# One step of a hybrid diffusion model with a mixture of experts: expert blocks of 32 tokens in four column groups, and every weight piece through a staging buffer

## What is computed

```
scores = sigmoid(x @ router_w);  sel = scores + router_b          # 16 experts in 4 groups
# the best group, in it the best 2 experts; weights = their scores, normed to sum 1
xb  = rows of x, sorted by expert
yb  = (silu(xb @ w_gate[e]) * (xb @ w_up[e])) @ w_down[e]         # 1024 -> 1024 -> 1024, f32
y   = for each token: sum of its 2 rows of yb, each by its weight
```

## Time and profile before

| | us |
|---|---|
| median of 3 runs | 1455.94 (1453.58 to 1458.22) |
| span of the profiled execution | 1449.7 |
| the profiled execution's own time | not told by the page; the median is 6.2 above the span |
| PE busy | 1358.5 (94% of the span) |
| PE L2222 (gates), L2233 (down) busy | 405.8, 212.7 |
| DVE, ACT, POOL busy | 433.9, 265.5, 234.1 |
| HBM | 282 MB read, 33 MB written |

### The profile page before, as it was taken

The page is one execution under the profiler, slowest core; times in us unless marked ns, Lnnn a source line. Parts: engine busy times, 40 slices in busy tenths (PEclk is TensorE's granted clock), DMA queues, the critical chain, the costliest instruction groups (busy, mean ns, idle before and its releaser), DMA issues.

```text
span 1449.7 us, 26021 instructions
## 1 busy us (share of the span) xinstructions
PE 1358.5 (94%) x10242; PEld 850.3 (59%) x10243; DVE 433.9 (30%) x913; ACT 265.5 (18%) x401; POOL 234.1 (16%) x280
## 2 busy tenths in 40 slices
PE   5898999978999999999969999999999999999975
PEld 3688778756787666664434455555555455554532
DVE  4792860375622412104462000000000000000065
ACT  3305012244125000000111111111111111111102
POOL 0043402200000000000005013003122222222320
PEclk9899899998999999999989999999999999999997
DMA  7459622345430212413168818917949999999993
GB/s 302 152 136 386 140 69 66 81 147 181 170 111 10 87 44 73 172 46 145 44 249 330 342 29 340 395 29 292 396 155 396 389 398 380 403 380 403 377 402 132
DMA packets 91756, 318.07 MB, mean 219 GB/s; under 512 B 11920, under 2 KB 12304, under 8 KB 91440
## 3 DMA queue, kind: packets, MB, share of 16 engines
q1 hardware_dynamic: 72304, 268.77, 48.9%
q0 software_dynamic: 10608, 34.19, 8.0%
q10 hardware_dynamic: 8784, 14.24, 3.2%
HBM read 281.99 MB, written 33.06 MB: 217 GB/s over the span
## 4 chain that ended last, share of the span: by engine, by line
PE 79%; DMA 8%; DVE 5%; issue 3%; ACT 2%; SPq 2%; POOL 0%; POOLq 0%; DVEq 0%; ACTq 0%
PE ps L2222 22%; PE ps L1762 11%; PE ps L2233 11%; PE ps L1750 10%; DMA expert_w<-in_w_down 5%; PE ps L2132 5%; PE ps L2183 4%; PE ps L1854 2%; PE ps L1937 2%; DMA expert_w<-in_w_up 2%; SPq L553 1%; PE ps L2228 1%; PE ps L2212 1%; PE ps L1777 1%; DMA x_sorted<-h,router_ints 1%
## 5 line engine op out<-in xcount | busy, mean ns | idle before, releaser
L2222 PE MATMUL ps<-expert_w,x_block_t 128*64 128x256 f32 x3584 | 405.8, 383 | 10.6 <-issue 6.7
L2222 PEld LDWEIGHTS ps<-expert_w,x_block_t 128*64 128x64 f32 x3584 | 257.2, 138 | 159.1 <-issue 33.7
L2233 PE MATMUL ps<-expert_w,act_t 128*64 128x512 f32 x896 | 212.7, 602 | 4.1 <-DMA expert_w<-in_w_down 3.7
L1762 PE MATMUL ps<-h_t,weight_ring 128*128 128x320 f32 x640 | 179.0, 436 | 0.1
L1762 PEld LDWEIGHTS ps<-h_t,weight_ring 128*128 128x128 f32 x640 | 121.6, 191 | 54.2 <-issue 7.6
L1750 PE MATMUL ps<-h_t,weight_ring 128*128 128x320 f32 x512 | 148.8, 454 | 2.8 <-ACT h_t L730 2.8
L1661 DVE TENSOR_TENSOR activations<-silu_tmp,ps 128x256 f32<-128x256 f32 x56 | 23.6, 422 | 375.7 <-ACT silu_tmp L948 375.6
L1750 PEld LDWEIGHTS ps<-h_t,weight_ring 128*128 128x128 f32 x512 | 102.0, 201 | 46.7 <-issue 9.3
L2233 PEld LDWEIGHTS ps<-expert_w,act_t 128*64 128x64 f32 x896 | 58.3, 137 | 101.4 <-issue 81.4
L673 POOL COPY expert_w<-staged 128x1024 f32<-128x1024 f32 x42 | 43.8, 1043 | 416.8 <-PE ps L2222 315.9
L1682 DVE COPY y_block<-ps 128x512 f32<-128x512 f32 x25 | 17.3, 692 | 187.5 <-PE ps L2233 187.5
(11 more groups left out here) (355 smaller groups left out, 1309.1 us busy)
## 6 DMA issues: line engine op xcount, KB each, us to landing
expert_w<-in_w_down SPq DMA_DIRECT2D x128, 512.0 KB, 13.6
weight_ring<-in_stream SPq DMA_DIRECT2D x98, 512.0 KB, 5.0
expert_w<-in_w_gate SPq DMA_DIRECT2D x58, 512.0 KB, 11.3
expert_w<-in_w_up SPq DMA_DIRECT2D x58, 512.0 KB, 12.3
staged<-in_w_gate SPq DMA_DIRECT2D x28, 512.0 KB, 13.9
gathered<-in_w_gate SPq DMA_DIRECT2D x28, 512.0 KB, 15.9
gathered<-in_w_up SPq DMA_DIRECT2D x28, 512.0 KB, 16.5
x_sorted<-zero POOLq DMA_DIRECT2D x18, 512.0 KB, 15.0
```

The source lines that it names most:

```text
L1762: last = mm(pair(job)[:, a, :], w[:, k, :], h_t[:, k, a * HALF:(a + 1) * HALF], start=(k == 0), stop=(k == KD - 1))
L2222: last = mm(ps[MB * g:MB * g + MB, 2 * half + w, 0:256], x_blk_t[:, 2 * kp + k2, :], rows[:, at_col:at_col + 256], start=(kp == 0 and k2 = ...
L2233: last = mm(ps[MB * half:MB * half + MB, 4, :], act_t[:, 4 * (f // 4) + 2 * (f % 2) + f // 2 % 2, :], w_slot[3 * f + 2][:, 4 * half:4 * ha ...
```

## The change

A block has MB = 32 rows. With the counts above that is 48 blocks (in the order of the experts 2, 7, 1, 7, 1, 5, 2, 4, 2, 3, 2, 3, 2, 3, 2, 2). PE runs each product in four column groups of 32 stationary columns and 256 moving columns. The transposes of x and of the activations are made by DVE (32x32 blocks, with the weights stored on the host in the matching order), so PE has no transposes in the loop and ACT no copies. The down product of a block runs one block later, after the gates of the next. All 24 pieces of an expert are staged in 8 buffers and copied by POOL; of the last expert, 16 are staged and the 8 of w_down go straight to their slots. The last 4 blocks are kept in `y_last`, and there are three buffers for gathered rows, which no longer serve as staging buffers. In the diff the parts of SP, POOL, ACT, DVE and PE follow in this order; `load_x` and `store_y` are four DMAs each, of 32 rows by 1 KB, and `add_some(n)` does n half rows of the gathered sum (a product or an addition).

```diff
-MB = 64
+MB = 32
-STAGED = 10
+FG = 4
+GW = D // FG
+LASTN = 4
+STAGES = 8
+PIECES = 3 * KF
...
+            for p in range(STAGES // 2, PIECES):
+                if p >= STAGES:
+                    sp.wait_ge(slot_filled, PIECES + (p + 1 - STAGES))
+                load_piece(second, p)
             with sp.Fori(2, EXPERTS - 1) as n:
-                next_expert(n, STAGED)
+                e = sp.value_load(rint[0:1, bass.ds(n + EXPERT, 1)], min_val=0, max_val=EXPERTS - 1)
+                for p in range(PIECES):
+                    sp.wait_ge(slot_filled, n * PIECES + (p + 1 - STAGES))
+                    load_piece(e, p)
+            for p in range(2 * KF):
+                sp.wait_ge(slot_filled, last_e * PIECES + (p + 1 - STAGES))
+                load_piece(e, p)
+            for f in range(KF):
+                sp.wait_ge(down_done, b * KF + (f + 1))
+                sp.dma_start(piece[2 * KF + f][:, :], w_experts[bass.ds(e, 1), 2 * KF + f, :, :].rearrange("a p n -> p (a n)"))\
+                    .then_inc(last_in[f], 16)
...
+            def fill(n, pieces):
+                b = pool.value_load(rint[0:1, bass.ds(n + START, 1)], min_val=0, max_val=NBLK)
+                for p in range(pieces):
+                    s = p % STAGES
+                    pool.wait_ge(stage_in[s], n * (16 * PIECES // STAGES) + 16 * (p // STAGES + 1 - PIECES // STAGES))
+                    pool.sem_inc(stage_full, 1)
+                    if p < 2 * KF:
+                        pool.wait_ge(gu_done, b * (2 * KF) + (p + 1))
+                    else:
+                        pool.wait_ge(down_done, b * KF + (p + 1 - 2 * KF))
+                    pool.sem_inc(slot_free, 1)
+                    nc.gpsimd.tensor_copy(piece[p][:, :], stage[s]).then_inc(slot_filled, 1)
+            with pool.Fori(1, EXPERTS - 1) as n:
+                fill(n, PIECES)
+            with pool.Fori(EXPERTS - 1, EXPERTS) as n:
+                fill(n, 2 * KF)
-            pool.wait_ge(y_stored, stored * 32 + 32)
+            pool.wait_ge(y_stored, limit * (16 * FG))
...
+            with act.Fori(2, NBLK) as i:
+                with act.If(i < limit):
+                    for h in range(2):
+                        act.wait_ge(gu_done, i * (2 * KF) + (h + 1) * KF)
+                        act.wait_ge(prod_ready, i * 2 + h)
+                        take_gate_half(h)
+                    act.wait_ge(xt_copied, i + 2)
+                    load_x(i * MB + 2 * MB)
+                    act.wait_ge(y_copied, i + 1)
+                    store_y(i * MB - MB)
...
+            with dve.Fori(2, NBLK) as i:
+                with dve.If(i < limit):
+                    dve.wait_ge(silu_ready, i * 2 + 1)
+                    take_prod(0)
+                    dve.wait_ge(x_blk_in, i * (16 * FG) + 16 * FG)
+                    dve.wait_ge(gu_done, i * (2 * KF) + 2 * KF)
+                    turn_x(x_blk[:, :])
+                    dve.wait_ge(silu_ready, i * 2 + 2)
+                    take_prod(1)
+                    dve.wait_ge(prod_ready, i * 2 + 2)
+                    dve.wait_ge(down_done, i * KF)
+                    turn_act()
+                    dve.wait_ge(y_stored, i * (16 * FG))
+                    copy_y()
...
+            for u, (beside, amid, behind) in enumerate(((0, 0, 4), (2, 3, 3), (2, 3, 3))):
+                take_prod(0)
+                add_some(beside)
...
+                turn_x(x_blk[:, :])
+                take_prod(1)
+                add_some(amid)
+                dve.wait_ge(down_done, limit * KF + u * KF)
+                turn_act()
+                take_last(u)
+                vec.nop().then_inc(y_copied, 1)
+                add_some(behind)
+            dve.wait_ge(down_done, limit * KF + (LASTN - 1) * KF)
+            take_last(LASTN - 1)
...
+            with pe.Fori(2, NBLK) as i:
+                with pe.If(i < blocks):
+                    pe.wait_ge(xt_copied, i + 1)
+                    gate_half(0, lambda p: pe.wait_ge(slot_filled, e * PIECES + (p + 1)))
+                    pe.wait_ge(prod_ready, i * 2)
+                    gate_half(1, lambda p: pe.wait_ge(slot_filled, e * PIECES + (p + 1)))
+                    pe.wait_ge(act_ready, i)
+                    pe.wait_ge(y_copied, i)
+                    down(lambda p: pe.wait_ge(slot_filled, before * PIECES + (p + 1)))
```

More of the change, by code:

```diff
@@ L238, in hybrid_step @@
[L238 to L243, removed]
+        rms2 = at("row_rms", gone + 24 * 320 + 3520 + 448, [P, 8 * CH])
+        rw = at("router_w_sb", gone + 24 * 320 + 3520 + 640, [P, KD, EXPERTS])
+        assert gone + 24 * 320 + 3520 + 640 + 512 <= small_end
@@ new lines, in hybrid_step @@
+        w_slot = [at(f"expert_w{s}", end - s * 4096, [P, D]) for s in range(PIECES)]
+        piece = [w_slot[n] for n in SLOT_OF]
+        pick_t = at("last_tokens_t", end - 3 * 4096, [P, CH, P])
+        x_blk = at("x_block", qs0, [P, GW])
+        x_blk_t = at("x_block_t", qs0 + 1024, [P, KD, MB])
+        act_t = at("act_t", qs0 + 2048, [P, KF, MB])
+        y_blk = at("y_block", qs0 + 3072, [P, GW])
+        silu = at("silu_tmp", qs0 + 4096, [P, P])
+        acts = at("activations", qs0 + 4608, [P, 2, P])
@@ L248, in hybrid_step @@
-        assert end + 8192 <= top[0] and len(stage) == STAGED and qs0 + 40960 <= end - 23 * 4096
+        stage = [at("staged0", end + 4096, [P, D])[:, :], sm[:, b_at:b_at + D]] \
+            + [at(f"staged{2 + i}", ring0 + 12288 + i * 4096, [P, D])[:, :] for i in range(3)] \
+            + [at(f"staged{5 + i}", qs0 + 5632 + i * 4096, [P, D])[:, :] for i in range(3)]
+        assert end + 8192 <= top[0] and len(stage) == STAGES and qs0 + 40960 <= end - 23 * 4096
         fin = [at(f"final{i}", pool0 + (10 + i) * 4096, [P, D]) for i in range(CH)]
@@ L325, in hybrid_step @@
         blocks_done = sem("blocks_done")
[L326 removed]
+        got_in = [sem(f"got_in{s}") for s in range(3)]
         pick_ready = sem("pick_ready")
@@ L573, in _ @@
+            for f in range(KF):
+                sp.wait_ge(last_in[f], 16)
+                sp.sem_inc(slot_filled, 1)
             for c in range(CH):
@@ L2238, in _, with down, landed @@
+            def down(filled):
+                for f in range(KF):
+                    filled(2 * KD + f)
+                    for g in range(FG):
+                        last = mm(ps[MB * g:MB * g + MB, 4, 0:GW], act_t[:, f, :], piece[2 * KD + f][:, GW * g:GW * g + GW],
+                                  start=(f == 0), stop=(f == KF - 1))
+                    last.then_inc(down_done, 1)
+            def landed(p):
+                pe.wait_ge(first_in[p], 16)
             pe.wait_ge(act_took, h2_job("L", CH - 1) + 1)
@@ L2254, in _ @@
[L2254 to L2264 removed]
+            gate_half(0, landed)
+            gate_half(1, landed)
+            pe.wait_ge(act_ready, 1)
@@ L2303, in _ @@
             last.then_inc(pick_turned, 1)
+            pe.wait_ge(act_ready, blocks)
+            pe.wait_ge(y_copied, blocks)
+            down(lambda p: pe.wait_ge(slot_filled, EXPERTS * PIECES + (p + 1 - PIECES)))
             pe.wait_ge(pick_taken, 1)
-            def add_last(c, u):
+            for c in range(CH):
                 cv = 0 if c < SCH else 1
-                pe.wait_ge(y_last_ready, 2 * u + cv + 1)
-                for half in range(2):
-                    rows = slice(MB * half, MB * half + MB)
-                    last = mm(ps[:, 2 * (c % 2) + half, :], pick_t[rows, u, c, :], y_last[rows, u, cv, :],
-                              start=(u == 0), stop=(u == 1))
-                return last
```

447 lines of the change are left out of this document (166 added, 281 removed).

## The result

| | before | changed |
|---|---|---|
| median, us | 1455.21 (1453.58 to 1458.22, 4 runs) | 1479.33 (1474.15 to 1485.02, 4 runs) |
| span of the profiled execution | 1449.7 | 1483.2 (its own time 1485.02) |

The ratio is 1.0181 (95% interval 1.0138 to 1.0223): slower by 24 us. The forecast was 1468, in the right direction and half as large (12 us); the time lies inside the range of 1443 to 1495 and that of the likeliest case, 1460 to 1482.

What follows compares the result with a forecast made beforehand. It took PE, then DMA, to bound the expert stage, DVE the end. Copy loop's end 1395 us (6 for the clock included), 67 for the end gives 1462, plus 6.2 gives 1468 us; range 1443 to 1495.

Steps and rivals of the forecast that it cites:

- a period above 11 us: Sign against the forecast: a block in the first large expert was to take 10.4 us on PE, not over 11.
- Copy loop's end: POOL's last weight copy: 1051 + 284.5 + 48 + 5 = 1389 us, with 6 us for the clock 1395.
- 192 x 0.054 = 10.4 us a block: PE's time for a 32-row block: 192 matmul records at 54 ns, no transposes and no wait for silu.
- a rival (11.7 us a block): Four column groups miss full pace, waiting at each piece: 61 ns a record, total 1490 us; chance 0.1.
- 864 + 52 + 5 x 10.4: Start of the second large expert's last gates: first large expert's at 864, 52 us step, five blocks; 968 us.
- 6 for the clock: PE at half clock after idle waits: 2 us at each of three PE-bound places, 6 us in all.
- From there DMA never waits: After the third large expert's last block starts, at 1051 us, DMA was to be busy without a pause.
- x and y at 2.0 us a block: DMA cost of a block's loads and stores: 2.0 us, bounds 1.2 and 3.0; 48 us over 24 blocks.
- The end, 67 us: From the copy loop's end at 1395: gathers, DVE's chain of sums to 1443, then the rest to 1462 us.
- the rival with a hidden tail: Gathered sums fit between PE's last blocks, so the end takes 57 us, not 67; total 1458 us; chance 0.14.
- 6.2 us around the span: The median was put 6.2 us above the profiled span: 1462 becomes 1468 us.
- The traffic goes by bytes: Rival: x and y cost DMA 1.2 us a block instead of 2.0; total 1446 us, faster; chance 0.2.

Runs made afterwards that it cites:

- the first series: The changed kernel as it is, first group of four runs against the kernel before: 1479.33 us, ratio 1.0181; run again later, 1476.61 us, ratio 1.0159.
- the late and the extra load: Two edits of the changed kernel: PE's second table load moved behind the gates, 1467.49 us; an unused third load at the loop's head, 1495.64 us.
- the five early gathers: The changed kernel with five gathers issued among the last expert's 16 copies: 1470.6 us, ratio 1.0099.
- four more buffers: The changed kernel with 12 staging buffers instead of 8: 1452.57 us, ratio 0.9984; with late load and five gathers too, 1429.46 us, ratio 0.9823.
- the other repairs: The changed kernel with PE's second load behind the gates, 1467.49 us, or five gathers among the last copies, 1470.6 us; both together 1454.76 us.

## Why the prediction was half right

The direction was right, and most of the mechanism; four terms of the copy loop's sum were not, and they left the forecast at 12 of the 24 us measured. The first of them, the loop turn, had no term at all, and the prediction had named a period above 11 us as a sign that it was wrong. By its own steps, in the profiled execution of the first series:

- **Copy loop's end, 1395 forecast, 1413.4 measured.** Four errors, two of which cancel.
  - *The loop turn was costed at nothing.* The step "192 x 0.054 = 10.4 us a block" has 11.45 in its place: 7, 5 and 3 blocks, 15 x 1.05 = 16 us. The last gates of the first large expert start at 873.2 instead of 864; 7.4 of these 9.2 us are the turn, the rest is the lower clock and late pieces in the first two blocks. Shown by the late and the extra load. The kernel before had one load and slower matmuls: its PE-bound blocks hid one load and two alike. I had the price as a rival (11.7 us a block) with 0.1, but for another reason.
  - *The small expert's down product was left out of the step* "864 + 52 + 5 x 10.4". The 52 held (51 us), but 6.2 and 5.6 us follow it: 12. I had put 6 for the clock instead, in all.
  - *"From there DMA never waits"* was wrong: some 12 us of standstill in the fourth large expert, and shorter dips later.
  - *x and y at 2.0 us a block* was too much; the DMA-bound stretch from 1078.0 took 335.4 us, and less 284.5 for the pieces, 12 of standstill and 5 for issue, landing and copy this leaves 33.9 / 24 = 1.4 a block. 24 x 0.6 is 14 us less. Of the 1.4 only 0.9 is the traffic, in its own queue; the rest is shorter dips and slower pieces, some 13 us in all for which the sum had no term. So the 338 us forecast for the stretch were right by two errors.
  - Sum: 1395 + 16 + 12 - 6 + 12 - 14 = 1415.
- **The end, 67 us.** 69.8 from the last copy's end, and not the 57 of the rival with a hidden tail. The mechanism was right: gathers behind the copies, DVE as the chain, x's transpose behind the rows. The trace shows the order, and the five early gathers show that their place costs time.
- **6.2 us around the span.** The changed kernel's profiled execution has 1485.02 - 1483.2 = 1.8. I took the difference between a median and another execution's span for a constant: 4.4 too much. 1468 + 18.4 + 2.8 - 4.4 = 1484.8.
- **Hidden as forecast:** DVE's transposes (0.44 us), ACT's eight DMAs, x's landing (median 5.0), POOL's copies.
- **The rivals.** "The traffic goes by bytes" was true, as the first rival had it, and the time was not its 1446, since the turn and DMA's standstill took more. The rule that stood beside it was that of the Trainium skill, "DMA: Bandwidth & Descriptors", section "Why small descriptors are slow (HBM only)". By that rule, 35/67 = 0.52, the trace agrees. Packets from 817 to 997 us in the changed kernel:

```profile
q10 hardware_dynamic: 5281, 3.61, 7.4%
```

Two thirds of the 5281 are data, and the small packets are again set at nothing: 0.074 x 16 x 180 / 3520 = 60.5 ns for 1 KB, against 115 for 2 KB, 0.53, and not the 0.76 of my line. (By bytes alone it would be 0.50; these rows hardly tell the two apart.)

## What to carry to other kernels

When a change halves the matmuls, whatever was hidden behind them has to be priced again: the loop turn with its register loads first. Put a load that only a later part needs ahead of that part, not at the head of the loop. Where two bounds take turns, what counts is how much work can be stored between them: four more buffers were worth more here than either of the other repairs. And take the price of traffic from its own queue's share, not from what is left over.

## What was not expected of the hardware

- A third load of a register at PE's loop turn cost 0.62 us and the second some 0.9, behind records of 54 ns; one cost nothing. Behind 128 gate records a load cost nothing, and 0.35 where PE had just waited for a piece. In the kernel before, with records of 107.9 ns, a second load cost nothing in the PE-bound blocks (period 22.46).
- DVE's operations with two operands in SBUF and POOL's copies slow each other: a product went from 1.28 to 1.81 us, an addition from 1.22 to 1.94, a copy from 1.04 to 1.5. That is the contention which the Trainium skill, "SBUF — State Buffer", section "SBUF: two separate sides", describes: a pair of ports that DVE and POOL share, and that one holds while the other waits; the trace agrees in that both get longer.
- A DMA issue of ACT for 32 rows of 1 KB took 0.45 us (four in 1.80); I had taken 0.6 from the earlier trace rows.
